# An expert loop on one core: each accumulator addition moved ahead of a weight pair's low part on VectorE

## The reference, cut to what matters

```
y = zeros
for e in range(16):
    a = silu(h @ w_g[e]) * (h @ w_u[e])          # 1024 -> 512
    y = y + gates[:, e:e + 1] * (a @ w_d[e])     # 512 -> 1024, float32
```

## Time and profile before

| | |
|---|---|
| median of 3 runs | 1906.4 us (1901.56 to 1916.81) |
| the profiled execution | 1912.61 us |
| its span, first to last instruction | 1910.7 us |
| mean granted TensorE clock | 0.963 of full speed |
| busy share of the span | TensorE 91%, VectorE 61%, ScalarE 50%, GpSimd 41% |

### The profile page before, as it was taken

The page is one execution under the profiler, slowest core; times in us unless marked ns, Lnnn a source line. Parts: engine busy times, 40 slices in busy tenths (PEclk is TensorE's granted clock), DMA queues, the critical chain, the costliest instruction groups (busy, mean ns, idle before and its releaser), DMA issues.

```text
span 1910.7 us, 23799 instructions
## 1 busy us (share of the span) xinstructions
PE 1746.1 (91%) x8427; PEld 1367.1 (72%) x8427; DVE 1160.1 (61%) x1449; ACT 947.6 (50%) x1333; POOL 775.1 (41%) x303
## 2 busy tenths in 40 slices
PE   6899999999979999999959999999998799999996
PEld 2677778767658777777736777877774677777774
DVE  2225556633457888888752363665344688888886
ACT  2344354443456666666533353534534466666662
POOL 1344544435123444444414454434450344444442
PEclk9899999999889999999979999999998799999998
DMA  8744343343558877787827344334432477778783
GB/s 288 270 144 117 115 121 89 113 155 111 177 176 263 256 255 256 250 259 255 272 96 258 98 133 122 91 97 133 135 111 99 161 256 249 255 256 254 255 269 124
DMA packets 187335, 353.22 MB, mean 185 GB/s; under 512 B 13414, under 2 KB 19048, under 8 KB 187244
## 3 DMA queue, kind: packets, MB, share of 16 engines
q1 hardware_dynamic: 169056, 319.09, 52.3%
q10 hardware_dynamic: 18188, 32.92, 4.9%
HBM read 348.30 MB, written 3.67 MB: 184 GB/s over the span
## 4 chain that ended last, share of the span: by engine, by line
PE 74%; DVE 14%; issue 5%; ACT 4%; DMA 2%; DVEq 1%; SPq 0%; ACTq 0%
PE ps L528 53%; PE ps L1030 5%; PE ps L537 4%; PE ps L1048 3%; DVE wxl L2179 3%; PE ps L556 2%; DVE pick L2185 2%; DVE y L2206 2%; PE ps L851 1%; PE ps L567 1%; DMA own<-w_mod 1%; ACT oe L1695 1%; PE ps L879 1%; PE ps L575 1%; PE ps L785 1%
## 5 line engine op out<-in xcount | busy, mean ns | idle before, releaser
L1748 POOL TENSOR_TENSOR wl<-raw,wh 128x1024 fp32r<-128x1024 f32 x168 | 409.7, 2442 | 569.3 <-ACT wh L1198 569.0
L1758 POOL TENSOR_TENSOR wxl<-raw,wxh 128x1024 fp32r<-128x1024 f32 x128 | 359.8, 2827 | 535.4 <-ACT wxh L1657 535.3
L1657 ACT ACTIVATE wxh<-raw 128x1024 fp32r<-128x1024 f32 x384 | 390.9, 1057 | 145.7 <-DMA raw<-w_e_down 114.3
L2179 DVE TENSOR_TENSOR wxl<-raw,wxh 128x1024 fp32r<-128x1024 f32 x256 | 379.9, 1511 | 1.8 <-ACT wxh L1657 1.6
L528 PE MATMUL ps<-wxh,xeT 128*128 128x512 f32 x1024 | 352.2, 396 | 15.2 <-DVE wxl L2179 11.1
L528 PE MATMUL ps<-wh,hTh 128*128 128x512 f32 x720 | 297.0, 413 | 4.4 <-DVE hTl L1819 2.6
L1198 ACT ACTIVATE wh<-raw 128x1024 fp32r<-128x1024 f32 x168 | 176.3, 1055 | 235.4 <-PE ps L528 234.6
L528 PE MATMUL ps<-wh,hTl 128*128 128x512 f32 x720 | 284.6, 395 | 0.0
L528 PE MATMUL ps<-wl,hTh 128*128 128x512 f32 x720 | 284.6, 395 | 0.0
L528 PEld LDWEIGHTS ps<-wxh,xeT 128*128 128x128 f32 x1024 | 195.2, 191 | 60.6 <-DVE wxl L2179 13.0
L528 PE MATMUL ps<-wxl,xeT 128*128 128x512 f32 x512 | 202.3, 395 | 0.0
(11 more groups left out here) (231 smaller groups left out, 2305.1 us busy)
## 6 DMA issues: line engine op xcount, KB each, us to landing
raw<-w_e_gate SPq DMA_DIRECT2D x128, 512.0 KB, 5.5
raw<-w_e_up SPq DMA_DIRECT2D x128, 512.0 KB, 4.3
raw<-w_e_down SPq DMA_DIRECT2D x128, 512.0 KB, 5.0
raw<-w_in SPq DMA_DIRECT2D x120, 512.0 KB, 3.8
own<-w_mod ACTq DMA_DIRECT2D x27, 1024.0 KB, 7.6
raw<-w_mod SPq DMA_DIRECT2D x42, 512.0 KB, 4.6
raw<-w_br_b SPq DMA_DIRECT2D x16, 512.0 KB, 3.7
raw<-w_out SPq DMA_DIRECT2D x16, 512.0 KB, 3.7
```

The costliest lines, as they stand in the source:

```text
L1657: act.activation(wxh[:, q % RING_MOE, :, :], raw[:, place, :, :], ACT.Copy).then_inc(sem("hi_done"), 1)
L1748: pool.tensor_tensor(wl[:, p % RING, :, :], raw[:, PAIR_CHUNK[p] % RAW, :, :], wh[:, p % RING, :, :].bitcast(F32), ALU.subtract).then_inc( ...
L1758: pool.tensor_tensor(wxl[:, q % RING_MOE, :, :], raw[:, expert_chunk(l, 0, q)[0], :, :], wxh[:, q % RING_MOE, :, :].bitcast(F32), ALU.subt ...
L2179: dve.tensor_tensor(wxl[:, q % RING_MOE, :, :], raw[:, expert_chunk(l, 0, q)[0], :, :], wxh[:, q % RING_MOE, :, :].bitcast(F32), ALU.subtr ...
```

## The change

Two lines of VectorE's program change places. In the loop over c, addition c is now issued ahead of low part 5+c. VectorE's order becomes: low part 4, addition 0, low part 5, addition 1, low part 6, addition 2, low part 7, additions 3 and 4, `ae`. The amount of work stays the same, and so do all waits and counts; no other engine's program changes. In expert 0, which has no additions, nothing changes.

```diff
@@ -2219,9 +2219,9 @@
                 if isinstance(e, int) and e == 1:
                     dve.wait_ge(sem("y_zero"), at("y_zero", l, 1))
                 for c in range(5):
-                    expert_lo(e, 5 + c)
                     if not first:
                         combine(e - 1, c)
+                    expert_lo(e, 5 + c)
                 dve.wait_ge(sem("silu_done"), at("silu_done", l, 1) + e)
```

## The result

The changed kernel takes 1925.28 us (median of 4 runs, 1922.89 to 1926.87) against 1907.38 us before; the ratio is 1.0088, with a 95% interval of 1.0045 to 1.0131. It is slower by 17.9 us, where 23.2 were forecast. The profiled execution took 1924.58 us, with a span of 1922.7 us.

What follows compares the result with a forecast made beforehand. TensorE's order was taken to set the time (busy 91%), other engines costing only where it waits. 28.8 - 8.8 + 3.2 = +23.2 us on the median 1906.4 gave 1929.6 us; range 1923 to 1936 (chance 0.70), wider 1915 to 1942.

Steps and rivals of the forecast that it cites:

- The reading of the long low parts: VectorE's and GpSimd's low parts exclude each other; VectorE's ends 1.09 us after GpSimd's, GpSimd's 2.27 us after VectorE's.
- Odd experts: 16 odd experts: low part 7 falls behind GpSimd's pair 9, pair 7 starts late; 1.80 us each, +28.8 us.
- TensorE's wait at pair 7: Sign in the profile after: one TensorE wait of about 1.7 us for a low part in each odd expert.
- The reading that pair 6 would be 0.1 us late: Odd experts: low part 6 done at 1733.17, TensorE wants it at 1733.09; 0.1 us late, counted as nothing.
- Even experts: 12 even experts, 2 to 12: chunk waits go, low parts come late, pair 7 starts earlier; 0.73 us each, -8.8 us.
- The waits at pairs 6 and 7: Sign in each even expert: two TensorE waits for low parts, 1.0 us at pair 6, 1.4 us at pair 7.
- Expert 14: Two experts without `pick` instructions, running like odd ones: pair 7 starts 1.6 us later each, +3.2 us.
- DMAs at nothing: Next expert's first pairs, issued later by SyncE, stay just covered; 0 to 0.3 us on ScalarE, nothing taken.
- (a): Rival: only the additions mattered; the 12 even experts fall to 22.73 us, 48 us less, 1858 us; chance 0.05.
- (b): Rival: same exclusion, but VectorE's low part 7 goes ahead of GpSimd's pair 9; 1880 us; chance 0.05.
- (c): Rival: GpSimd's pair 8 gets in ahead of low part 5 in even experts, nothing gained there; 1939 us; chance 0.08.
- The chances: Whole kernel: slower by more than 1% (above 1925.5 us) 0.68, within 1% 0.22, faster 0.10.

Runs made afterwards that it cites:

- after_again: The changed kernel timed once more beside the kernel before: 1927.0 us against 1905.5, ratio 1.0107.
- hold9: Changed kernel, with GpSimd's low part of pair 9 also waiting for VectorE's low part 7: 1881.3 us, ratio 0.9867 to the kernel before.
- late_pick: Kernel before, with the six `pick` instructions of an even expert moved from the head to behind addition 3: 1866.8 us, ratio 0.9812.

## Why the prediction was right

The time, 1925.3 us, lies in the lower part of the range of 1923 to 1936, and the direction was forecast. The two ends of the terms would give 1923 to 1934, so by its own terms the upper bound stood 2 us too high. By its steps:

- **The reading of the long low parts** as turns of two engines, with a cadence of 1.09 and 2.27 us, held: 1.08 and 2.25 us after the change, and 1.08 us with GpSimd's instruction at half its columns.
- **Odd experts**: +1.80 us each forecast, +1.77 measured. Pair 7 was late as worked out: counted from the `ae` before it, it starts at 22.72 us, where 22.78 was worked out and 21.10 was the time before. One sign was put down wrongly: TensorE's wait at pair 7 was to be about 1.7 us, and the row has 1.22. Of the difference, 0.16 us is the way a row counts (next point); the rest is that TensorE had already lost 0.13 us waiting for low part 6 and 0.14 us in restarting behind it. The reading that pair 6 would be 0.1 us late held too: it starts at 1736.90, where its pace from pair 5 at 1734.96 would have been 1736.77.
- **Even experts**: -0.73 forecast, -0.80 measured. The waits at pairs 6 and 7 were forecast at 1.0 and 1.4 us; the rows have 0.84 and 1.24. A row counts from the end that it gives the multiplication before, 0.39 us after its start, while at TensorE's pace the next one starts 0.23 us after it. Counted from that pace, pair 6 at 1712.38 is 1.00 us late and pair 7 at 1715.73 is 1.40 us late, as forecast.
- **Expert 14**: +1.6 forecast, +1.60 in layer 0 and +1.40 in layer 1. In after_again it was +2.60 and +1.70.
- **DMAs at nothing**: held for TensorE. For ScalarE it did not: 0 to 0.3 us was put down, and its waits for the gate pairs grew by 0.8 us each. None of it reached TensorE, but the size was not foreseen.
- **The sum**: 23.2 forecast, 21.6 in the loops, 17.9 and 21.5 between medians in two comparisons. No term is off by more than 1 us: odd experts 16 x 0.03 = 0.5 us too high, even ones 12 x 0.07 = 0.8, expert 14 0.2. What remains to the 17.9 us was not traced to a place; executions differ by more than that outside the loops (last section).
- **The rivals**: (a) fell, since the waits for additions went and low parts took their place. (b) did not happen, pair 9 was queued in time in all 16 odd experts; hold9, which forces it, gives 1881 us. (c) did not happen either, even experts all lie at 25.98 to 26.12 us.
- **The chances**: I put 0.68 on slower by over 1%. The first comparison says 0.88%, so what came is what had 0.22; the second says 1.07%. The border runs through the effect, and on which side a comparison falls is chance.

## What to carry to other kernels

When an instruction has two very different durations, look at which other engine is busy in the long ones before moving anything: a wait table names the additions that came late, not the low parts ahead of them that blocked. Where two engines exclude each other, the order of instructions on one of them also decides who meets whom; write both engines' ends down as one chain and see which instruction falls behind one more turn. A wait added to the engine that has time, so that it yields to the one on the path, was worth 2.3% here, for two lines. The best new order on that path, late_pick, gave 1.9%, and the intervals of the two touch. Both together were not tried.

## What the runs showed of the hardware

Subtractions of two SBUF operands on VectorE and on GpSimd never ran together. In the 13 traces 608 of VectorE's low parts took more than 1.3 us. Every one of them had met one of GpSimd's, and ended 1.08 to 1.09 us after that one's end, whether GpSimd's had 1024 columns or 512. The other way round, GpSimd's ended 2.22 to 2.29 us after VectorE's, and with 512 columns 1.13 to 1.25. The experiments show the exclusion and that it scales with the holder's duration. That its seat is a port pair to SBUF is what the Trainium skill states ("SBUF — State Buffer", "SBUF: two separate sides"), and no run here tests the seat.

The 115 ns of that page of the Trainium skill are measured, by its own words, on the descriptors of a DMA that wait for VectorE; the prediction took the figure over to two blocked subtractions. With a whole instruction of 1.22 us it would have given 1.33 us after the holder's end. The rows have 1.08, so a blocked instruction is quicker to its end than that sum. How, no run shows.

The part ahead of the expert loops differs between executions by more than this change is worth in one layer. Over the 13 traces the first `ae` starts between 568.8 and 581.5 us: at 581.53 in the trace before, at 570.72 in the one after and at 574.01 in after_again, with nothing changed there. Read a change's worth from the stretch that it touches, and use the medians as the check.
